# First layer: the first head's turn in front of the next tile's scores

## The reference

```
layer 0:  x = x + even_mixer(rmsnorm(x, a0_norm));   x = x + swiglu(rmsnorm(x, f0_norm))
layer 1:  x = x + odd_mixer(rmsnorm(x, a1_norm));    x = x + swiglu(rmsnorm(x, f1_norm))
return rmsnorm(x, final_norm)
```

```
s = einsum('bhrnqd,bhrnkd->bhrnqk', qb, kb) * (HEAD_DIM ** -0.5)   # scores, then penalty or bias
p = exp(s - m);  l = sum(p);  o = einsum('bhrnqk,bhrnkd->bhrnqd', p, vb) / l
```

## Time and profile before

| what | value |
|---|---|
| median of 3 runs | 2527.78 us (2526.22 to 2528.99) |
| span of the profiled execution | 2521.2 us |
| its own time with what lies around the span | not recorded apart; the runs' median lies 6.6 us above the span |
| PE busy | 2496.5 us, 99% |
| PEld busy | 2058.5 us, 82% |
| DVE busy | 1765.8 us, 70% |
| ACT busy | 1152.4 us, 46% |
| mean granted TensorE clock | 0.998 of full speed |
| where the change acts | about 60 to 490 us from the span's start |

### The profile page before, as it was taken

The page is one execution under the profiler, slowest core; times in us unless marked ns, Lnnn a source line. Parts: engine busy times, 40 slices in busy tenths (PEclk is TensorE's granted clock), DMA queues, the critical chain, the costliest instruction groups (busy, mean ns, idle before and its releaser), DMA issues.

```text
span 2521.2 us, 34920 instructions
## 1 busy us (share of the span) xinstructions
PE 2496.5 (99%) x12891; PEld 2058.5 (82%) x12891; DVE 1765.8 (70%) x2655; ACT 1152.4 (46%) x2012; POOL 410.9 (16%) x317
## 2 busy tenths in 40 slices
PE   9999999899999999999999999999999999999998
PEld 7888877688888888888888888888888888888887
DVE  6556565656878878666577777777657888887655
ACT  6555654535333333444455454546344333334433
POOL 1001022400332333100000000000002333332000
PEclk9999999999999999999999999999999999999999
DMA  3122253723444444866211111111334444447754
GB/s 130 59 60 77 60 129 99 216 93 117 155 171 163 150 168 167 315 219 211 81 48 49 50 50 50 48 50 72 117 109 144 164 157 162 157 160 255 246 194 152
DMA packets 189171, 332.38 MB, mean 132 GB/s; under 512 B 59728, under 2 KB 67792, under 8 KB 180816
## 3 DMA queue, kind: packets, MB, share of 16 engines
q1 hardware_dynamic: 154208, 320.62, 37.1%
q10 hardware_dynamic: 34800, 9.60, 1.7%
HBM read 238.24 MB, written 91.91 MB: 131 GB/s over the span
## 4 chain that ended last, share of the span: by engine, by line
PE 96%; DVE 2%; ACT 1%; issue 1%; DMA 0%; POOL 0%; ACTq 0%; SPq 0%; DVEq 0%
PE PS L2422 21%; PE PS L2337 19%; PE PS L2339 19%; PE PS L2338 19%; PE PS L2586 5%; PE PS L2518 4%; PE PS L2542 3%; PE PS L2534 1%; PE PS L2489 1%; PE PS L2563 1%; PE PS L2345 1%; PE PS L2436 1%; PE PS L2567 1%; PE PS L2503 1%; PE PS L2479 1%
## 5 line engine op out<-in xcount | busy, mean ns | idle before, releaser
L2422 PE MATMUL PS<-HH,WS 128*128 128x512 f32 x1536 | 516.0, 402 | 3.4 <-DVE HL L1641 2.0
L2422 PEld LDWEIGHTS PS<-HH,WS 128*128 128x128 f32 x1536 | 285.6, 188 | 60.0 <-DVE HL L1641 2.1
L2422 PE MATMUL PS<-HL,WS 128*128 128x512 f32 x768 | 301.9, 393 | 0.0
L2126 DVE TENSOR_TENSOR SPLIT<-RAWI,SPLIT 128x1024 fp32r<-128x1024 f32 x154 | 195.3, 1271 | 148.2 <-ACT SPLIT L1469 147.7
L1469 ACT ACTIVATE SPLIT<-RAWI 128x1024 fp32r<-128x1024 f32 x154 | 163.0, 1060 | 206.8 <-PE PS L2339 151.9
L2337 PE MATMUL PS<-TH,WS 128*128 128x512 f32 x640 | 249.2, 389 | 0.7 <-ACT SIL L1461 0.7
L2338 PE MATMUL PS<-TL,WS 128*128 128x512 f32 x640 | 249.0, 389 | 0.0
L2339 PE MATMUL PS<-TH,WS 128*128 128x512 f32 x640 | 249.0, 389 | 0.0
L2337 PE MATMUL PS<-SPLIT 128*128 128x512 f32 x616 | 240.0, 390 | 0.0
L2339 PE MATMUL PS<-SPLIT 128*128 128x512 f32 x616 | 239.7, 389 | 0.0
L2338 PE MATMUL PS<-SPLIT 128*128 128x512 f32 x616 | 239.6, 389 | 0.0
(11 more groups left out here) (274 smaller groups left out, 4957.9 us busy)
## 6 DMA issues: line engine op xcount, KB each, us to landing
WR<-wstrips SPq DMA_DIRECT2D x224, 256.0 KB, 2.7
RAWI<-ab_scratch SPq DMA_DIRECT2D x154, 256.0 KB, 4.2
ab_scratch<-SIL SPq DMA_DIRECT2D x132, 256.0 KB, 2.0
WD<-wdown SPq DMA_DIRECT2D x22, 1024.0 KB, 7.4
wd_scratch<-WD SPq DMA_DIRECT2D x22, 1024.0 KB, 3.8
RAWI<-wd_scratch SPq DMA_DIRECT2D x88, 256.0 KB, 3.3
UR<-wstrips SPq DMA_DIRECT2D x80, 256.0 KB, 3.1
RAWI<-wdown SPq DMA_DIRECT2D x66, 256.0 KB, 3.8
```

The costliest lines, as they stand in the source:

```text
L2126: e.tensor_tensor(SPLIT[m % 6][:, 1], RAWI[:, m % 4], f(SPLIT[m % 6][:, 0]), ALU.subtract).then_inc(S["ilo"], 1)
L2422: last = e.matmul(ps, wt, xt, start=g == 0, stop=g == 23)
```

## The change

In these 39 tiles PE issues the next tile's scores behind the first head's turn instead of at the tile's head. In the even dilated tiles the scores so come behind `pv(*last, 0)` too. No instruction is added or taken away, and no other engine's program changes.

```
                 values_first = P == 4 and n == 0
-                if after and not late_scores and not values_first:
+                turn_first = (P, n) != (0, 0) and (n < NQ - 1 if kind == "A" else n % 2 == 1 and n < NQ - 1)
+                if after and not late_scores and not values_first and not turn_first:
                     qk(*after)
                 if P == 0 and n == 1:
                     tv(*first.pop(0), P, n)
...
                 if values_first:
                     qk(*after)
                 turn(P, n, 0, kind)
+                if turn_first:
+                    qk(*after)
                 if P == 0 and n == 0:
```

## The result

The changed kernel takes 2544.75 us (median of 5, 2541.91 to 2546.11) against 2527.78 us before (2526.22 to 2528.99). The ratio is 1.0075, with a 95% interval of 1.0063 to 1.0086: 17 us slower. The forecast was 2543.3 us, slower by 15.5 us, with a range of 2534 to 2552.

What follows compares the result with a forecast made beforehand. The prediction took PE, busy 99% of the span, to bound the kernel. Its terms, 1.0 + 8.6 + 1.3 + 3.9 + 0.4 + 0.3 = 15.5 us, on 2527.8 gave 2543.3 us, range 2534 to 2552.

Steps and rivals of the forecast that it cites:

- What bounds the kernel: PE, busy 99% of the span; the dilated pairs have hardly any PE wait that an earlier turn could remove.
- The seams: Idle time between 64-row and 128-row matmuls on PE: 0.04 us more per odd dilated tile, 1.0 us for 24 odd tiles.
- The rival in which shorter seams save time: Scores behind 128-column transposes save 0.19 us in each of 39 tiles, -7.4 us, giving 2520 us; chance 0.03.
- y_add late: Even dilated tiles: head 1's values wait for y_add behind ttr, 8.6 us in pairs 0 to 2, 1.3 in pair 3.
- The late value batch: Pairs 0 to 2: head 0's values wait for their batch, 3.9 us in tile 4, 0.4 us in tile 2.
- Local tiles: Only the seam counts in pairs 4 to 6; pair 7, tile 1, lacks cover and loses 0.3 us, between 0 and 0.6.
- The clock falls too: Rival: each of 18 new PE waits brings a fall of TensorE's clock, 25 us more, 2568 us; chance 0.06.

Runs made afterwards that it cites:

- e1: The changed kernel with the new order in the 24 odd tiles alone, the even dilated tiles as before; ratio 1.0002 to the kernel before.
- e2: The changed kernel with head 0's y_add put ahead of the next tile's ttr on DVE in even dilated tiles; ratio 1.0032 to the kernel before.
- e4: The changed kernel with the scores between values and turn of head 0 in even dilated tiles; ratio 1.0043 to the kernel before.
- e7: The changed kernel with y_add ahead of ttr on DVE and PE's old order in tile 4 of pairs 0 to 2; ratio 1.0016 to the kernel before.
- e6: The kernel before with the new order in the 15 even dilated tiles alone, all odd tiles in the old order; ratio 1.0062 to it.
- e9: The changed kernel with DVE's two weight splits of pair 3 moved behind the next tile's ttr and head 0's lo; one run, 2542.0 us against 2526.9 before.
- e3: The changed kernel with four fills moved ahead of head 1's values in even dilated tiles of pairs 0 to 2; 2538.93 us, ratio 1.0042 to before.
- e5: The changed kernel with y_add ahead of ttr, old PE order in tile 4 of pairs 0 to 2 and tiles 2, 6 of pair 3; ratio 1.0006 to before.
- e8: The kernel before with DVE's weight split of pair 7, tile 5, moved behind tile 6's ttr, y_add and lo; 2524.04 us against 2526.06, ratio 0.9991.

## Why the prediction was right, by its own steps

- **What bounds the kernel.** Right. PE had no waits in the stretch that could be removed, and every wait added to it came out at the end: 17.6 us in the dilated pairs, 17 us in the runs.
- **The seams, +1.0 us.** Right in kind, over in size: e1 shows 0.2 us in the dilated stretch for 12 odd tiles, 0.02 each where 0.04 was counted. The rival in which shorter seams save time is out: idle time in front of the scores did fall to 0.17 us, and the sum stayed.
- **y_add late, 8.6 + 1.3 us.** Right. The steps are 0.8 us in pairs 0 to 2 and 0.3 to 0.4 in pair 3; e2, which takes this one cause away, gives 16.9 - 7.1 = 9.8 us for the forecast's 9.9. e4 confirms the count at a second distance.
- **The late value batch, 3.9 + 0.4 us.** Right: 3.7 us for tile 4 by e2 and e7. Tile 2's 0.1 us can't be told from tile 6's step.
- **Missed: lo of head 0 in pair 3, 2.9 us.** The forecast said that values of head 0 at the tile's head wait for the value batch, and took every other input as ready. It read one odd tile of pair 2, where no weight split stands ahead of that `lo`. In pair 3 tiles are shorter and the split comes one tile earlier in the queue. e6 shows that the even tile's own order uncovers it, e9 that the split is what makes it late.
- **Missed: tv in pair 0, tile 1, 0.7 us.** The forecast priced every odd tile by one of pair 2, at the seam alone. This one has a `tv` at its head, the scores were its cover, and a second `tv` waits on DVE behind `ttr`. The kernels with and without the new order in this tile show it, 5.11 against 4.40 us.
- **Local tiles, 0.3 us.** Nothing from 306 to 479 us in the changed kernel (0.1 us); behind that, pair 7's end differs by 0.7 us, in a place where the kernels of the experiments differ from before by -0.03 to 3.7 us, and where they also differ in which DVE instructions run beside a GpSimd operation (last section). It stays open whether 0.3 us of it is the change.
- **The clock falls too.** It didn't in the changed kernel: in 60 to 330 us the granted clock is 1.00 with all 16 waits at L2563 in it. But the rival is not an empty one: in e3 one fall came behind the wait in pair 0, tile 1, for 1.0 us.

```profile
60.00:330.00 270.00, 257.61 (x1609) 210.35 (x1606) 150.81 (x430) 149.65 (x410) 22.37 (x25) 1.00 0.21 57
```

So the main terms were right by their mechanism: 9.8 and 3.7 us measured for 9.9 and 3.9. That the sum came so near is in part luck. Two missed terms, 2.9 and 0.7 us, stand against small terms that came out lower: 0.8 us at the seams, up to 0.4 us in tile 2, and 0.3 us in pair 7.

## What to carry to other kernels

When the first engine issues a step later, look at the other engines' queues for what stands behind the instruction that waits for that step: here one `y_add` behind four `ttr`, whose own input had been ready for 2.7 us. Count the wait as two sums from one common event, the follower's queue and the first engine's own work until it needs the result, and do it for each kind of tile, since a split of weights ahead of two tiles of pair 3, and a `tv` at the head of the first changed tile, were what I overlooked. Moving cover to a wait takes it from another place, and moving a slow step in a queue may only move the wait.

## What the runs showed of the hardware

- The idle time in front of matmuls on 64 rows depends on what was before: 0.36 us after a fill of 512 columns, 0.17 us after a transpose of 128. After them it is 0.22 us in either order. The sum over a tile did not change with the order.
- Two weight splits on DVE take 1.28 us in most places and 3.45 us beside a GpSimd operation on 128x1024 at pair 7's end, in the kernel before:

```profile
485.52 3.45 DVE L1619 TENSOR_TENSOR WS<-WR,WS 128x512 fp32r<-128x512 f32 x2
...
485.82 5.36 POOL L987 TENSOR_TENSOR Y<-Y,YQ 128x1024 f32<-128x1024 f32 x2 [0.84 <-DMA YQ<-l_scratch]
```

  In the changed kernel the same two splits both start ahead of the GpSimd operation, and take 1.48 us:

```profile
502.28 1.48 DVE L1619 TENSOR_TENSOR WS<-WR,WS 128x512 fp32r<-128x512 f32 x2
...
503.72 4.66 POOL L987 TENSOR_TENSOR Y<-Y,YQ 128x1024 f32<-128x1024 f32 x2 [1.11 <-DMA YQ<-l_scratch]
...
504.74 0.54 DVE L1863 TENSOR_TENSOR ATB<-PS,ATB 128x384 fp32r<-128x384 f32 x1
...
506.64 2.82 DVE L2011 TENSOR_TENSOR HL<-YE,HH 128x1024 fp32r<-128x1024 f32 x1
```

  Over all eleven traces, twelve splits at pair 7's end start while L987 runs (in before, e1, e2, e3, e5, e8 and e9). Each of them ends 0.55 to 0.56 us after that operation, whenever it started; one alone takes 0.68 us. The subtractions of 128x1024 (HL from YE and HH) that start under it all end 1.08 to 1.09 us after it. `lo`, which reads PSUM and SBUF, runs beside it in 0.54 us, as above. So DVE waited until GpSimd was done. The Trainium skill, SBUF — State Buffer, section "SBUF: two separate sides", tells of a port pair that DVE and GpSimd hold one at a time for a whole instruction, when DVE reads two operands from SBUF and the GpSimd operation reads SBUF. The traces agree with it. In e8 the first split starts at 489.07, 0.06 us behind the second L987, so moving the split moved the wait.
- The clock fell at pair 7's end behind PE's long idle stretch: 0.50 in 508 to 512 us of the changed kernel, behind 504 to 508 with 0.82 of 4.00 us busy, as in the earlier trace rows. In e3 it fell behind a much shorter one as well: 0.72 in 60 to 64 us, behind 56 to 60 with 2.83 of 4.00 us busy. In the changed kernel the same stretch has 2.84 of 4.00 us, and the clock stayed at 1.00. So what one stretch looks like does not tell whether the clock falls.
